# Hybrid decoder step on one core: one small step-size job moved behind the fourth convolution tile, with its consumer on VectorE and two SiLUs on ScalarE

## The reference, cut to what matters

```python
proj = hn @ w_in
z, xbc, dt_raw, u5, gate_a, gate_b = jnp.split(proj, IN_PROJ_SPLITS, axis=-1)
xbc_c, new_conv = causal_depthwise_conv(xbc, conv_buf, conv_w, conv_b)   # 4 taps, then silu
...
dt = jax.nn.softplus(dt_raw.astype(jnp.float32) + ssd_dt_bias.astype(jnp.float32))
a = -jnp.exp(ssd_a_log.astype(jnp.float32))
y_ssd, new_ssd = ssd_chunked_scan(xh, dt, a, bm, cm, ssd_h0)
...
y_s5, new_re, new_im = s5_scan(u5, s5_re0, s5_im0, ...)
...
return merged @ w_mix_out, new_conv, new_ssd, new_re, new_im
```

## Time and profile before

| | before |
|---|---|
| median of three runs | 1082.95 us |
| the profiled execution's own time | 1083.02 us |
| its span, first to last instruction | 1081.3 us |
| PE busy | 949.8 us (88%) |
| DVE busy | 477.4 us (44%) |
| ACT busy | 326.9 us (30%) |
| granted TensorE clock, mean | 0.94 of full |
| DMA | 297.70 MB, mean 275 GB/s |

### The profile page before, as it was taken

One profiled execution on the slowest core, in us unless ns is written; L12 is line 12 of the kernel. 1 busy time (PEld: TensorE's weight loads), 2 busy tenths in 40 slices (PEclk: granted clock), 3 DMA queues, 4 the chain that ended last, 5 costly groups with the idle time before them and its releaser, 6 DMA issues.

```text
span 1081.3 us, 16067 instructions
## 1 busy us (share of the span) xinstructions
PE 949.8 (88%) x6661; PEld 627.5 (58%) x6661; DVE 477.4 (44%) x804; ACT 326.9 (30%) x652; POOL 53.9 (5%) x82
## 2 busy tenths in 40 slices
PE   6999999999999999999999999786768587678565
PEld 4778478995589999989877654231313223132121
DVE  5998965666777445655665310202001020201014
ACT  4143155566466245553543511000000000000003
POOL 2601400010100000000000000000000000000000
PEclk9999999999999999999999999988868888897888
DMA  9582450344463743525799879999999999999994
GB/s 271 136 186 74 152 194 2 127 149 152 137 214 123 302 161 116 204 79 178 284 358 345 309 286 419 422 421 422 422 422 421 422 422 421 423 422 422 423 416 154
DMA packets 92868, 297.70 MB, mean 275 GB/s; under 512 B 21101, under 2 KB 31049, under 8 KB 69116
## 3 DMA queue, kind: packets, MB, share of 16 engines
q1 hardware_dynamic: 90468, 289.33, 69.9%
q0 software_dynamic: 2112, 7.28, 2.0%
q10 hardware_dynamic: 216, 0.06, 0.0%
HBM read 286.76 MB, written 9.90 MB: 274 GB/s over the span
## 4 chain that ended last, share of the span: by engine, by line
PE 60%; SPq 33%; DVE 2%; issue 2%; ACT 1%; DMA 1%; POOL 1%; DVEq 0%; ACTq 0%; POOLq 0%
SPq L647 31%; PE bank L1393 7%; PE bank L1378 6%; PE bank L1775 5%; PE bank L1777 5%; PE bank L1776 5%; PE bank L2106 3%; PE bank L1402 3%; PE bank L2155 2%; PE bank L1666 2%; PE bank L1565 2%; PE bank L1786 2%; SPq L645 2%; PE bank L1787 1%; PE bank L1788 1%
## 5 line engine op out<-in xcount | busy, mean ns | idle before, releaser
L2106 PE MATMUL bank<-ring,work 128*32 128x512 f32 x704 | 131.8, 684 | 35.2 <-DMA ring<-in_w_exp_up_dram 22.5
L1775 PE MATMUL bank<-ops,usplit 128*128 128x320 f32 x368 | 114.5, 311 | 1.1 <-DVE usplit L2587 1.1
L1776 PE MATMUL bank<-ops,usplit 128*128 128x320 f32 x368 | 113.9, 309 | 0.0
L1777 PE MATMUL bank<-ops,usplit 128*128 128x320 f32 x368 | 113.8, 309 | 0.0
L2124 PE MATMUL bank<-ring,work 128*32 128x512 f32 x352 | 75.0, 827 | 40.1 <-DMA ring<-in_w_exp_down_dram 29.6
L2106 PE MATMUL bank<-work 128*32 128x512 f32 x256 | 85.7, 691 | 13.4 <-DMA work<-in_w_exp_up_dram 6.6
L2587 DVE TENSOR_TENSOR usplit<-ring,usplit 128x2048 fp32r<-128x2048 f32 x31 | 71.0, 2290 | 52.9 <-ACT usplit L1080 52.9
L2106 PEld LDWEIGHTS bank<-ring,work 128*32 128x32 f32 x704 | 31.1, 123 | 99.3 <-issue 53.0
L1393 PE MATMUL bank<-work,ring 128*128 128x320 f32 (+1 forms) x304 | 77.4, 411 | 0.0
L2912 DVE TENSOR_TENSOR work<-bank,g 128x512 f32<-128x512 f32 x8 | 5.5, 692 | 161.6 <-PE bank L2155 161.6
L1080 ACT ACTIVATE usplit<-ring 128x2048 fp32r<-128x2048 f32 x32 | 61.5, 1921 | 40.5 <-PE bank L1777 31.6
(11 more groups left out here) (493 smaller groups left out, 1719.9 us busy)
## 6 DMA issues: line engine op xcount, KB each, us to landing
ring<-in_w_exp_gate_dram SPq DMA_DIRECT2D x46, 1024.0 KB, 25.7
ring<-in_w_exp_down_dram SPq DMA_DIRECT2D x43, 1024.0 KB, 26.4
ring<-in_w_exp_up_dram SPq DMA_DIRECT2D x41, 1024.0 KB, 25.9
ring<-in_w_in_dram SPq DMA_DIRECT2D x11, 2048.0 KB, 9.5
work<-in_w_exp_up_dram SPq DMA_DIRECT2D x16, 1024.0 KB, 26.0
work<-in_w_exp_gate_dram SPq DMA_DIRECT2D x14, 1024.0 KB, 25.7
work<-in_w_exp_down_dram SPq DMA_DIRECT2D x14, 1024.0 KB, 26.0
ring<-in_w_glu_dram SPq DMA_DIRECT2D x4, 2048.0 KB, 8.9
```

The source lines that it names most:

```text
L1775: nc.tensor.matmul(b[:, 0:T], wh, hi_[:, k], start=(k == 0), stop=False)
L1776: nc.tensor.matmul(b[:, 0:T], wh, lo_[:, k], start=False, stop=False)
L1777: ins = nc.tensor.matmul(b[:, 0:T], wl, hi_[:, k], start=False, stop=(k == KT - 1))
L2106: ins = nc.tensor.matmul(psum[part][ES * x:ES * (x + 1), :], xs[i % 2][:, kk, x], wt[x][:, k], start=(kk == 0), stop=(kk == KT - 1))
```

## The change

`dt3` moves one place down the list, behind `xbc3`, and its matmuls move on PE behind the four tiles. With that, `xbc3` and `dt3` exchange banks. On DVE the four instructions that read `dt3` move from between the second and the third convolution tile to behind the fourth `block_taps`. On ACT the SiLU of tiles 0 and 1 moves: each now stands between `conv_in` and `first_tap` of the tile two further on, where it stood one tile earlier behind `first_tap`.

```diff
-    j += ["xbc0", "xbc1", "dtT", "xbc2", "dt3", "xbc3"]
+    j += ["xbc0", "xbc1", "dtT", "xbc2", "xbc3", "dt3"]
...
                 if m == 2:
                     states_back(1)
                     act.wait_ge(s["sls"], 1)
+                if m >= 2:
+                    conv_silu(m - 2)
                 first_tap(m)
                 if m == 1:
                     got(act, "dtT")
                     emptied(act.activation(dtS, bank("dtT")[:, 0:T], ACT.Copy), "dtT")
-                if 1 <= m < 3:
-                    conv_silu(m - 1)
...
-                if m == 2:
-                    b = take("dt3")
-                    done(pe, "dtT")
-                    ...
-                    end(ins, "dt3")
+            b = take("dt3")
+            done(pe, "dtT")
+            ...
+            end(ins, "dt3")
...
             for m in range(4):
                 conv(m)
-                if m == 1:
-                    got(dve, "dt3")
-                    ...
-                    TT(dte, dtx, dtm, ALU.min).then_inc(s["dtx"], 1)
...
             for ft in range(6):
                 block_taps(ft)
+                if ft == 3:
+                    got(dve, "dt3")
+                    dve.wait_ge(s["ld_small"], 16 * 8)
+                    TT(dtx[:, 0:2], bank("dt3")[:, 0:32].rearrange("p (c n) -> p c n", c=2),
+                       dtb[:, :].unsqueeze(1).to_broadcast([P, 2, HEADS]), ALU.add)
+                    emptied(TT(dtx[0:NS, 2], bank("dt3")[0:NS, 32:48], dtb[0:NS, :], ALU.add), "dt3")
+                    done(dve, "dt3")
+                    q(TS(dtm, dtx, -1.0, None, ALU.mult))
+                    TT(dte, dtx, dtm, ALU.min).then_inc(s["dtx"], 1)
```

More of the change, by code:

```diff
@@ L1523, in _ @@
                     end(ins, "dtT")
-                if m == 2:
-                    b = take("dt3")
-                    done(pe, "dtT")
-                    for c in range(NC):
-                        R = ROWS[c]
-                        ins = nc.tensor.matmul(b[0:R, HEADS * c:HEADS * (c + 1)], dtS[:, P * c:P * c + R], fold4[:, :], start=True, stop=True)
-                    end(ins, "dt3")
+            b = take("dt3")
+            done(pe, "dtT")
+            for c in range(NC):
+                R = ROWS[c]
+                ins = nc.tensor.matmul(b[0:R, HEADS * c:HEADS * (c + 1)], dtS[:, P * c:P * c + R], fold4[:, :], start=True, stop=True)
+            end(ins, "dt3")
             def chunk_out(n_):
```

## The result

The changed kernel takes 1088.43 us in the median (1087.50 to 1090.42, 4 runs), the kernel before, beside it on the same chip, 1082.84 us (1080.73 to 1083.02, 4 runs). Over all paired runs the ratio is 1.0062, 95% interval 1.0044 to 1.0082: slower by 6.7 us (4.8 to 8.9). Over all 31 executions of the changed kernel on record the median is 1089.38. Of all timed runs in this document one is left out of the ratios, 1225.90 us at a mean granted clock of 0.74, a run of the kernel with nine extra calls. The profiled execution of after took 1089.66 us, with a span of 1087.9 us against 1081.3 before: 6.6 us.

What follows compares the result with a forecast made beforehand. The prediction took PE to bound the kernel up to about 630 us, then the saturated expert stream that PE's progress starts. It summed 1083.0 + 0 (PE) + 0 (ACT) + 4.6 (stall) + 2.0 (clock) = 1089.6 us, range 1086.9 to 1091.8.

Steps and rivals of the forecast that it cites:

- PE's work moved: 0: On PE, dt3's six matmuls (0.66 us) have no wait around them, so moving them gains nothing by itself: 0.
- ACT: 0: ACT's reshuffled SiLUs and table load before DVE's fourth tile cost nothing, hidden by DVE's 2.21 us wait: 0.
- Stall: 4.6: PE waits ahead of fy0, from 158.60 to 163.2, until DVE empties bank 1: 4.6 us, bounds 4.3 to 6.5.
- Clock: 2.0: PE behind the stall runs at clock 0.50 for a while, costing 2.0 us; bounds zero to 2.75.
- Nothing absorbed: Between PE's delay and the saturated expert stream starting at 630.18 no slack lies, so the end moves with it.
- The sum: Whole kernel: 1083.0 + 0 + 0 + 4.6 + 2.0 = 1089.6 us.
- The possible gain at 614.5: Half-clock stretch from 614.5 to 617.6 on PE may be spared by a shifted start: up to 1.5 us gained.
- The clock holds: Rival 1: behind the stall ahead of fy0 the clock stays up, only the stall counts: 1087.6 us, chance 0.20.
- Absorbed: Rival 2: the stall is taken in later, for example by the expert stream starting by itself: 1083.0 us, chance 0.07.
- not slower: Rival 4: bank 1 is free before yo1 ends, no stall, half-rate stretch at 614.5 spared: 1081.4 us, chance 0.02.
- The table load: Rival 3: ACT's table load delays DVE's fourth tile up to 1.9 us, long half-clock stretch: 1092.3 us, chance 0.09.

Runs made afterwards that it cites:

- the kernel with nine extra calls: Kernel before with only DVE's dt3 read moved late, plus nine unread matmul calls in PE's standstill: 1089.68 us, ratio 1.0064.
- the late load: Changed kernel with the 2 MB weight load issued when dt3 ends, not xbc3: 1091.12 us, ratio 1.0082; with seven extra matmul calls too: 1085.34 us, 1.0036.
- the ACT-only kernel: Kernel before with only the two SiLUs on ACT moved: 1082.42 us, ratio 1.0001.
- the one with DVE alone moved: Kernel before with only DVE's dt3 read moved behind the fourth block-diagonal matrix; dt3 then holds the bank yo1 takes next: 1092.62 us, ratio 1.0095.

## Why the prediction was right

- **PE's work moved: 0.** Right as a sum, incomplete as an account. It counted nothing else as moved with `dt3`. It also moves the load that hangs on `xbc3`, and that opens the gap. What a moved step releases on other queues has to be counted too. In the changed kernel the gap lies inside the stall and costs nothing there (the late load made it no faster); with the stall gone it costs 1.5 us in the trace (1.0018 against 0.9995).
- **ACT: 0.** Right: 1.0001 for it alone. Less the 0.87 us of upstream offset, the taps started at 151.52 and 153.48 (forecast 151.3 and 153.6), DVE's fourth tile at 154.29 (154.33) and its first matrix at 156.75 (156.75). That the cover is thin was right too: in the ACT-only kernel DVE's idle time ahead of that matrix is zero.
- **Stall: 4.6.** Measured 4.63, and 4.63 again in the two kernels with the late load. Its cause, the emptying of the inherited bank by DVE behind four matrices, is shown from both sides: another bank or an earlier read removes it, one matrix less shortens it by 1.52 us, another inherited job makes it 6.56.
- **Clock: 2.0.** The mechanism was right, the size too small: 2.76 in the changed kernel, at the upper bound of 2.75, and 4.39 with the wait in one piece, outside it. The term was a mean over six waits of the expert part, of which three had less than 4 us of work at half rate. The longest was the better guide; this is its stretch of the earlier trace rows from where the clock fell:

```profile
822.70:829.50 6.80, 5.48 (x28) 1.38 (x32) 0.00 (x0) 0.00 (x0) 0.00 (x0) 0.50 1.02 423
```

It is at half for 6.80 us, as are the changed kernel and the one with DVE alone moved. What is lost is nearly half of the time that PE works in it (2.76 of 5.77 us, 2.39 of 4.96), and that time depends on how long PE still stands after the clock has fallen: 1.3 us there, 1.0 in the changed kernel, 1.8 with DVE alone moved, whose wait was longer (6.49 us) and whose loss was smaller (2.39). The Trainium skill's rule in "TensorE: Matmul & The Clock Gate", "Part 1: The HAM clock gate", that idling drops the array to 1.2 GHz, agrees with the rows behind the long stalls.
- **Nothing absorbed.** Right: 6.73 us at the stream's start became 6.6 of span, and local sums and ratios agree through the table.
- **The sum.** 1089.6 forecast, 1088.43 measured, 1089.66 in the profiled execution. That the last meets the forecast to 0.1 us is luck: 0.8 too little for the clock and 0.87 upstream stand against the 1.5 us spared at 614.5. The medians' difference of 5.6 us is below the local 7.4 though inside the interval. The possible gain at 614.5, which the prediction named and did not count, was 1.5 us in the profile of after; but that stretch is missing in seven of the fourteen profiles, that of the ACT-only kernel among them, so it is not tied to the change.
- **Rivals.** "The clock holds" was 1087.6. The ratio's interval reaches down to 1.0044, about 1087.5 us, so the time alone doesn't rule it out; the granted clock of 0.50 from 163.0 does. "Absorbed" and "not slower" fell with the ratio. The table load did not reach DVE's fourth tile, as the tile's start shows.

## What to carry to other kernels

When a job changes its place in a rotation of PSUM banks, ask of its new bank who empties it and what stands ahead of that instruction, on an engine that may have nothing to do with the change: that distance, minus the work up to the bank's next job, is the stall. Add the clock to any stall of several microseconds on a dense PE (here 2.4 to 4.4 us on top of 4.6 to 6.6), and take the longest stretch at half rate in the trace as a guide to its price and not as a bound: here one was half as long again. And list the transfers that hang on a moved step's end, since here a large load issued half a microsecond earlier went with a late packet of code and a gap on PE.

## What was not expected of the hardware

- A 2 MB load issued 0.46 us ahead of `ye0`, instead of 0.10 behind, goes with a gap of 0.93 to 1.63 us on PE some 6 us later, for which the profile names no cause ("issue"). The instruction queue's packet is then 4.1 to 4.7 us behind the load instead of 0.8 to 1.0, and PE goes on 2.4 to 2.5 us behind the packet. Of the fourteen profiled executions the eight with the load behind had none, the six with it ahead all had one; in two of the eight the 64 matmuls start so late, at 163.94 and 165.18, that such a gap could not have shown.
- How much clock a stall costs does not follow its length: 2.8 us behind 0.93 and 3.23, 4.4 behind 4.56 in one piece, 2.4 behind 6.49 in one piece. Waits of 1.34 and 1.30 us close together cost none. All of this is one profiled execution each.
- Stretches of 3.5 us at half rate come and go between executions of kernels that do not differ there: near 81 us in 9 of the 14 profiles and near 615 to 628 us in 7, with about 1.5 us lost each (3.93 us of matmuls take 5.48 at 81 us). One profiled pair can differ by some 3 us for this alone, which is nearly half of the effect measured here.
